# Two-block layer kernel: attention turns, exponents and casts moved; norms summed per token; a joint norm; half a gate product on ScalarE

## The reference

```python
# first block, on 16 meta tokens + x
xn = rmsnorm(h, ln1_w);  proj = xn @ w_in        # dq dk dv | gq gk gv gr | gate ranks
da = rmsnorm(softmax(q1 k1) v - lam * softmax(q2 k2) v) * 0.8          # 4 heads
go = rmsnorm(gated_linear_attention_both_ways(gq, gk, gv, g)) * silu(gr)   # 4 heads
h = h + concat(da, go) @ w_out;  h = h[16:]
hn = rmsnorm(h, ln2_w)
h = h + peer(hn)       # 8 heads pick 16 of 16384 experts per token: sum gate * gelu(hn . u) * v
x = rmsnorm(h, final_norm_w)
# second block
h = rmsnorm(x, mix_norm);  z = h @ w_in_2        # pool | u, v | two gates
y_a = (windowed means of z_pool, 2 4 8 16 wide, @ w_pool) * scale @ w_branch_a
y_b = (gelu(u) * (w_spatial @ rmsnorm(gelu(v)) + b)) @ w_branch_b
x = x + (sigmoid(g_a) * y_a + sigmoid(g_b) * y_b) @ w_out_2
x = x + conv_ffn(rmsnorm(x));  x = x + sigmoid(rmsnorm(x) @ w_ple_gate) * (p @ w_ple)
return rmsnorm(x, final_norm)
```

## Time and profile before

| | us |
|---|---|
| median of 3 runs | 2437.65 (2434.55 to 2437.88) |
| profiled execution | 2438.38 |
| its span | 2436.6 |
| mean granted clock of TensorE | 0.984 of 2.4 GHz |

### The profile page before, as it was taken

How to read it: one execution, slowest core, us unless ns; L and a number is a source line. 1 busy time by engine, 2 the same in 40 slices (tenths; PEclk the granted TensorE clock), 3 DMA queues, 4 the chain that set the end, 5 groups by cost and what they waited for, 6 DMA issues and landing times.

```text
span 2436.6 us, 38068 instructions
## 1 busy us (share of the span) xinstructions
PE 2334.8 (96%) x13568; PEld 1298.9 (53%) x13568; DVE 1700.0 (70%) x2984; ACT 1053.1 (43%) x1496; POOL 535.7 (22%) x418
## 2 busy tenths in 40 slices
PE   7999899999999998899999999988999989999998
PEld 3446774555555566655555555563444444443454
DVE  5326775578899989978888888868353447776235
ACT  4265442666666654543333333344422233332233
POOL 0001001567788631124222222104000010000001
PEclk9998999999999999999999999999999999999998
DMA  5200012487899669899999999913233323332321
GB/s 179 78 27 1 1 57 92 144 287 289 302 324 343 226 228 331 326 336 361 377 363 361 363 356 362 343 53 113 78 113 100 100 87 96 103 97 96 100 86 52
DMA packets 164871, 470.79 MB, mean 193 GB/s; under 512 B 17616, under 2 KB 70736, under 8 KB 163984
## 3 DMA queue, kind: packets, MB, share of 16 engines
q1 hardware_dynamic: 109312, 289.59, 34.9%
q0 software_dynamic: 36864, 134.23, 14.8%
q10 hardware_dynamic: 18576, 45.36, 4.9%
HBM read 421.67 MB, written 47.45 MB: 193 GB/s over the span
## 4 chain that ended last, share of the span: by engine, by line
PE 82%; DVE 12%; issue 2%; ACT 2%; DMA 1%; POOL 1%; DVEq 0%; SPq 0%; ACTq 0%; POOLq 0%
PE psum L536 25%; PE psum L537 24%; PE psum L538 24%; DVE arena L2043 2%; PE psum L426 1%; DVE arena L510 1%; DVE arena L2081 1%; DVE arena L2078 1%; DVE arena L2082 1%; PE psum L990 1%; PE psum L876 1%; PE psum L962 1%; DMA arena<-in_urows,arena 1%; PE psum L850 0%; DVE arena L2079 0%
## 5 line engine op out<-in xcount | busy, mean ns | idle before, releaser
L536 PE MATMUL psum<-arena 128*128 128x384 f16 (+2 forms) x3648 | 1261.3, 347 | 35.1 <-DVE arena L467 13.2
L537 PE MATMUL psum<-arena 128*128 128x384 f16 (+2 forms) x3648 | 1264.5, 347 | 0.0
L538 PE MATMUL psum<-arena 128*128 128x384 f16 (+2 forms) x3648 | 1257.7, 346 | 0.0
L536 PEld LDWEIGHTS psum<-arena 128*128 128x128 f16 x3648 | 354.2, 97 | 367.1 <-issue 51.2
L538 PEld LDWEIGHTS psum<-arena 128*128 128x128 f16 x3648 | 353.9, 97 | 324.0 <-issue 8.1
L537 PEld LDWEIGHTS psum<-arena 128*128 128x128 f16 x3648 | 353.6, 97 | 311.8 <-issue 8.1
L510 DVE SCALAR_TENSOR_TENSOR arena<-arena 128x1024 f16<-128x1024 f32 x216 | 268.2, 1244 | 297.6 <-ACT arena L497 297.1
L497 ACT ACTIVATE arena<-arena 128x1024 f16<-128x1024 f32 x216 | 226.1, 1050 | 255.9 <-PE psum L538 243.8
L1622 ACT ACTIVATE arena<-arena 128x1024 f16<-128x1024 f32 x128 | 135.3, 1057 | 299.8 <-PE psum L538 285.8
L516 POOL TENSOR_TENSOR arena<-arena 128x1024 f16<-128x1024 f32 x104 | 214.4, 2061 | 105.4 <-ACT arena L505 104.4
L438 POOL TENSOR_TENSOR arena<-arena 128x512 f32<-128x512 f32 x15 | 19.8, 1321 | 918.4 <-ACT arena L393 918.4
(11 more groups left out here) (251 smaller groups left out, 2179.7 us busy)
## 6 DMA issues: line engine op xcount, KB each, us to landing
arena<-in_w SPq DMA_DIRECT2D x320, 512.0 KB, 3.6
arena<-in_v SPq DMA_DIRECT2D x128, 512.0 KB, 6.0
early_activations<-arena ACTq DMA_DIRECT2D x124, 192.0 KB, 5.1
arena<-early_activations SPq DMA_DIRECT2D x124, 192.0 KB, 5.9
gate_matrix<-arena ACTq DMA_DIRECT2D x5, 4096.0 KB, 16.1
arena<-gate_matrix SPq DMA_DIRECT2D x32, 640.0 KB, 8.0
arena<-in_xT SPq DMA_DIRECT2D x4, 512.0 KB, 6.0
arena<-in_urows,arena POOLq DMA_INDIRECT x128, 6.9
```

What stands on the lines that cost most here:

```text
L536: nc.tensor.matmul(ps, a_h, b_h, start=first, stop=False)
L537: nc.tensor.matmul(ps, a_h, b_l, start=False, stop=False)
L538: return nc.tensor.matmul(ps, a_l, b_h, start=False, stop=last)
```

## The change

- Norms: the squares become the weights and a few columns the moving side, so that each token's sum lands in its own row and the result has 4 or 5 columns (`pick`). Root and reciprocal work on those; TensorE spreads the inverse by a broadcast column times the identity, now for the first norm too. There VectorE adds squares 3 to 7; one of three weight cuts goes behind the reciprocal.
- final1 and mixn are one `Norm`: with s1 and s2 the mean squares of the input and of the input times the weight, the factor of the second norm is computed from both (`wpick`, `w12`, `moments`), in one pass. Its sums for chunks 0 to 5 stand inside the last `expert_output`. The multiply that makes the first block's output X runs in the first pool projection.
- Scores, maximum, exponential and difference of turns 0 and 1 run between the gate projections. The gate is 1 + tanh(x/2) for twice the sigmoid, with the half in a later factor.
- The first two exponents use free banks (1 and 3) and run between the last turns.
- In head 0 the head norm only scales; cast and subtraction of the four heads run in the first eight steps of head 1. The wide product waits for the scaling alone.
- In the gate rows VectorE makes the low product for four of the eight tokens, ScalarE the other four with one activation each (`low_half`), for the octet ahead.
- Pool projections run from the last chunk to the first; four slabs of gating values come between them and the pool products, whose results go into U2 instead of V2.

```diff
 N_PQ = 32
 N_U = 48
 N_POOL = N_U + NK
-N_WP = N_POOL + 8
-N_SV = N_WP + 4
-N_SU = N_SV + 8
+N_SV = N_POOL + 8
+N_WP = N_SV + 4
+N_SV2 = N_WP + 4
+N_SU = N_SV2 + 4
...
-                if self.meta:
-                    nc.tensor.matmul(bank(self.b), ones, self.sq[:, c, 0:T], start=c == 0, stop=c == KC - 1)
-                    last = nc.tensor.matmul(bank(self.b + 1, M), ones, self.sq[:, c, T:TM], start=c == 0,
-                                            stop=c == KC - 1)
+                end = c == KC - 1 or c == self.lo and self.hi == KC - 1
+                for t in (0, *range(TT, self.tiles), *range(1, TT)):
+                    rows = P if t < TT else M
+                    w = wpick[:, c, 6 - 2 * t:14 - 2 * t] if self.double else pick[:, TT - t:TT - t + self.n]
+                    last = nc.tensor.matmul(bank(self.sums, self.n)[0:rows], self.squares[:, c, t * P:t * P + rows], w,
+                                            start=first and t == 0, stop=end and t == TT - 1)
+                if end:
+                    last.then_inc(ss_done, 1)
...
+            def add_squares(self, eng, op):
+                for c in range(self.lo + 1, self.hi + 1):
+                    eng.wait_ge(sq_act, self.i * KC + c + 1)
+                    if c > self.lo + 1:
+                        eng.wait_ge(squares_added, self.before + c - self.lo - 1)
+                    op.tensor_tensor(self.sq[:, self.lo, 0:self.cols], self.sq[:, self.lo, 0:self.cols],
+                                     self.sq[:, c, 0:self.cols], ALU.add).then_inc(squares_added, 1)
...
+                pe.wait_ge(inv_done, self.i + 1)
+                for at, b in ((TT, self.b), (0, self.b - 1)) if self.double else ((0, self.b),):
+                    for t in range(self.tiles):
+                        rows = P if t < TT else M
+                        last = nc.tensor.matmul(psum[:, b * 512 + t * P:b * 512 + t * P + rows],
+                                                self.inv[0:rows, at + t:at + t + 1].to_broadcast([rows, P]),
+                                                ident[0:rows, 0:rows], start=True, stop=True)
+                    last.then_inc(spread_done, 1)
...
+                if self.double:
+                    dve.wait_ge(ss_done, self.i + 1)
+                    s1, s2 = (bank(self.sums, self.n)[:, j:self.n:2] for j in range(2))
+                    dchain.link(nc.vector.tensor_scalar(moments[:, 0:TT], s1, EPS, None, ALU.add))
+                    dchain.link(nc.vector.scalar_tensor_tensor(out=moments[:, TT:2 * TT], in0=moments[:, 0:TT], scalar=EPS,
+                                                               in1=s2, op0=ALU.mult, op1=ALU.add))
+                    nc.vector.reciprocal(self.std, moments).then_inc(std_done, 1)
                 else:
...
-            return psum[0:rows, (6 + n % 2) * 512:(7 + n % 2) * 512]
+            b = 6 + n % 2 if n >= 2 else 1 + 2 * n
+            return psum[0:rows, b * 512:(b + 1) * 512]
...
+                pe.wait_ge(gate_out, 1 + (n - N_GR + 1))
+                chunk(pe, n, slot(n), bank(4 + n - N_GR))
+                if n == N_GR + 1:
+                    pe.wait_ge(proj_out, 4)
+                    scores(0)
+                elif n == N_GR + 2:
+                    scores(1)
+            for turn in range(2, HEADS * TT):
...
+            exponents(0)
+            turn_over(HEADS * TT - 1)
+            mix_values(HEADS * TT - 2)
...
+            exponents(1)
             mix_values(HEADS * TT - 1)
-            pe.wait_ge(turn_out, HEADS * TT)
-            exponents(0)
-            pe.wait_ge(av_out, HEADS)
-            exponents(1)
...
-                    pe.wait_ge(mixl_out, 1)
+                    pe.wait_ge(head_scaled, HEADS)
...
+                pe.wait_ge(low_out, e + 1)
...
+                        if c >= 2:
+                            n4.sum(pe, c - 2)
                 if not last:
...
+            pe.wait_ge(final1_out, KC)
+            gating_values(N_SV)
+            pe.wait_ge(zpool_out, KC)
+            for n in range(N_WP, N_SV2):
+                p = n - N_WP
+                g = N_SV2 - 1 - n
...
+            gating_values(N_SV2)
...
+                nc.scalar.activation(sgr[:, n - N_GR, :], bank(4 + n - N_GR), ACT.Tanh, scale=ISW / 2).then_inc(sig_out, 1)
+                if 1 <= n - N_GR <= 2:
+                    turn_exp(n - N_GR - 1)
...
+            turn_copy(HEADS * TT - 2)
             step_exp(0)
+            turn_copy(HEADS * TT - 1)
...
+            step_exp(1)
+            head_out(HEADS - 1)
...
+            def low_half(e):
+                b = e % 2
+                act.wait_ge(hot_slab_out, e + 1)
+                wait(act, g_done, e * 2 - 2)
+                for j in range(OCT // 2, OCT):
+                    tok = e * OCT + j
+                    last = nc.scalar.activation(hot_low[b][:, j // QUAD, :, j % QUAD],
+                                                hot_slab[b][:, j // QUAD, :, j % QUAD], ACT.Copy,
+                                                scale=idxT[:, 2, tok:tok + 1])
+                last.then_inc(low_out, 1)
...
+                    if t * OCT + i + 1 < GT * OCT:
+                        low_half(t * OCT + i + 1)
...
+                dve.wait_ge(sig_out, n - N_GR + 1)
+                nc.vector.scalar_tensor_tensor(out=sgr[:, n - N_GR, :], in0=sgr[:, n - N_GR, :], scalar=1.0,
+                                               in1=bank(4 + n - N_GR), op0=ALU.add,
+                                               op1=ALU.mult).then_inc(silu_out, 1)
+                if 1 <= n - N_GR <= 2:
+                    scores_max(n - N_GR - 1)
+                    difference(n - N_GR - 1)
+            for turn in range(2, HEADS * TT):
...
+                scaled = nc.vector.scalar_tensor_tensor(out=o, in0=o, scalar=w, in1=bank(h),
+                                                        op0=ALU.mult, op1=ALU.mult)
+                if k == 0:
+                    scaled.then_inc(head_scaled, 1)
+                    return
+                dchain.link(scaled)
...
+                    if h == 1 and p < 2 * HEADS:
+                        head_cut(p // 2, p % 2)
...
+                nc.vector.tensor_tensor(hot_low[b][:, 0:half], hot_slab[b][:, 0:half], col(gatel)[:, 0:half],
+                                        ALU.mult).then_inc(hot_out, 1)
             def tile_turn(t):
...
+                    dve.wait_ge(spread_done, n4.i + 2)
+                    for cc in range(KC):
+                        nc.vector.scalar_tensor_tensor(out=X[:, cc, 0:T], in0=X[:, cc, 0:T], scalar=f1[:, cc:cc + 1],
+                                                       in1=bank(n4.b - 1), op0=ALU.mult,
+                                                       op1=ALU.mult).then_inc(final1_out, 1)
...
```

More of the change, by code:

```diff
@@ L366, in build @@
         xn_done, xh_done, xl_done = sem("xn_done"), sem("xh_done"), sem("xl_done")
-        POOLED, FIRST = ("ln2", "ffnn", "final2"), 6
         squares_added = sem("squares_added")
-        NORMS = ("ln1", "ln2", "final1", "mixn", "ffnn", "plen", "final2")
+        NORMS = ("ln1", "ln2", "mixn", "ffnn", "plen", "final2")
+        ADDED = {"ln1": (3, 7), "ln2": (0, 5), "ffnn": (0, 5), "final2": (0, 5)}
         def roots_table(i):
@@ L375, in build, with __init__ @@
         class Norm:
-            def __init__(self, name, b):
+            def __init__(self, name, b, sums=None):
                 self.i = NORMS.index(name)
[L380 to L383, removed]
+                self.b, self.sums = b, b if sums is None else sums
+                self.w, self.meta, self.double = VEC[name], name == "ln1", name == "mixn"
+                self.cut = name != "final2"
                 self.cols = TM if self.meta else T
[L386 to L389, removed]
+                self.tiles = TT + 1 if self.meta else TT
+                self.n = 2 * TT if self.double else self.tiles
+                self.lo, self.hi = ADDED.get(name, (KC, KC))
+                self.before = sum(ADDED[x][1] - ADDED[x][0] for x in NORMS[:self.i] if x in ADDED)
+                self.sq = nsq1 if self.meta else nsq
+                self.squares = xsq if self.double else self.sq
+                self.std = (nstd1 if self.meta else nstd)[:, 0:self.n]
+                self.inv = (ninv1 if self.meta else ninv)[:, 0:self.n]
             def square(self, c):
-                nc.scalar.activation(self.sq[:, c, 0:self.cols], X[:, c, 0:self.cols],
+                nc.scalar.activation(self.squares[:, c, 0:self.cols], X[:, c, 0:self.cols],
                                      ACT.Square).then_inc(sq_act, 1)
@@ L412, in sum @@
                 first = c == 0
[L413 to L414 removed]
+                if self.lo <= c <= self.hi:
+                    if c < self.hi:
                         return
[L416 to L417 removed]
+                    pe.wait_ge(squares_added, self.before + self.hi - self.lo)
+                    c, first = self.lo, self.lo == 0
                 else:
@@ L2332, in _ @@
```

(2 more changed lines are left out.)

357 lines of the change are left out of this document (173 added, 184 removed).

## The result

The changed kernel takes 2412.3 us (four runs, 2406.3 to 2417.2) against 2437.7 before: ratio 0.990, interval 0.9885 to 0.991. In a second series it took 2406.9 (2405.1 to 2411.2). It is faster, by 25 to 31 us, where 53 were predicted: both medians lie above the predicted 2385 and above the end of its range (2372 to 2402). The profiled execution took 2406.3, the fastest of the first four: its span is 2404.6, 32.0 less than before.

A forecast was written before the change was run, and what follows sets the result against it. TensorE, busy 96% of the span, bounds most stages; its idle time and the slow clock behind it can be won. Terms from norms to pool order sum to -52.8 us, from 2438.4 to 2385.6, forecast 2385; range 2372 to 2402.

The forecast's parts named there:

- Norms: Root and reciprocal on few columns shorten ln2, ffnn and final2 by 0.95 us each, -2.9 together; plen 0.
- TensorE's sum costs the same, 0.23 us each: In the norms' sums, a square matrix loaded as weights with 4 columns moved is no cheaper than 128 moved.
- First norm: At the kernel's start: shorter root and reciprocal and earlier sums, less a new spread and reordered weight cuts: -4.5 us.
- early turns: Start of attention: scores 0 and 1 between gate projections make the stretch to turn 5 12.3 instead of 20.6 us: -8.
- Early exponents and first head: Gated attention: earlier exponents give -2 us; casts and subtractions leaving the first head give -7, 1.5 of 8.5 left.
- Head 1: Second head of the gated attention: the casts and subtractions moved there cost +1 us, bounds 0 and +4.5.
- rival (c): VectorE gives gains back in head 1 (4.5 us of casts) and the pool projections (4.9 of multiplies): 2393; chance 0.12.
- Gate rows: VectorE's halved low product saves 2.1 us per tile, 12.8 in six; taken as -8, bounds 0 and -12.8.
- VectorE's 31.6 becomes 29.4 to 29.5: Gate-row tile: VectorE's time falls to this many us and stays the pace, as TensorE needs 28.3 without its waits.
- Rival (a): The gate rows gain nothing, because in-order ScalarE or the transfers become their pace: 2393 us; chance 0.18.
- Joint norm: Two norms before the pool mixer become one, with sums of chunks 0 to 5 inside the last expert: -12.8 us.
- rival (b): The clock stays at 2.4 GHz after the shorter norms, where it fell before: 2375 us; chance 0.12.

The follow-up runs named there:

- The run with late turns: The changed kernel with the first two attention turns back behind the gate projections, all else kept: 2418.4 us, ratio 0.9917.
- the last kernel: Changed kernel with 128-column sums, ring at word 3974, VectorE making octet 0's whole low product, octet 4's dot product before its low cut: 2386.6 us.
- `wide`: The changed kernel with the sums of ln2, plen, ffnn and final2 moving 128 columns instead of 4: 2399.5 us; three later kernels keep this.

## Why the prediction was wrong

The direction and most mechanisms were right, 2385 was not: 27 us off the first median. By the trace, 32.0 instead of 52.8 were won. Two steps failed by most: the sum with 4 columns moved, priced like the one with 128 (6.4 us lost at plen), and the query heads, taken as untouched because their code was (5.6 lost). Two more terms were too large, the gate rows by 3.7 us and the first gated head with its exponents by 2.8. Step by step:

- *Norms:* -3.6 for ln2, ffnn and final2 together against -2.9. But "TensorE's sum costs the same, 0.23 us each" and "plen: 0" failed, and this is one of the two large errors: at plen a square matrix loaded with 4 columns moved took 12.1 us for what 128 columns did in 7.4, +6.4 with what follows. The price of a weight load came from a row at full clock. I had priced the edit by duration at a given clock, and the clock was what it changed. At ln2 and the final norm it cost too, up to 2.4 and 1.6 us by the run with 128 columns there, hidden in a part that still came out as forecast.
- *First norm* -4.1, *early turns* -7.7 in the trace against -4.5 and -8. The first is the best of the executions: in the second profile of the same program it is -2.9. The run with late turns bears the second out. Of the table loads ahead of the first exponential (1.28 us each) one is gone, as the prediction had it: the tanh left the exponential's table in place.
- *Early exponents and first head:* -5.2 for -8. VectorE did start 4.2 us earlier (its first exponent product at 241.5, before at 257.5 less the 11.8 of shift), and the casts did leave. But it then waited 5.5 us for TensorE inside the head, where it had waited 3.4, and TensorE's wait for the wide scores fell from 4.37 to 2.00 only. The "1.5 that I leave" of 8.5 had to be more: an engine that runs ahead meets the other half of the loop. Head 1 lost 0.4 (predicted 1), so rival (c) didn't come there. In the second profile it lost 3.4, because the clock fell in it.
- *Query heads:* no step of the prediction named them, and they lost 5.6. Nothing in their code changed; their addresses did.
- *Gate rows:* -4.3 for -8. Small activations cost 0.29 start to start and VectorE's half 0.33, both as estimated. The failed step is "VectorE's 31.6 becomes 29.4 to 29.5", which let its idle time stay as it was. VectorE's work did shrink by 2.1 us per tile, but its wait in order for one cut, which nobody needed yet, grew from 0.83 to 1.61, and the tile won 1.1; 2.1 us at the start, TensorE's wait for ScalarE's first half, were not in the sum at all. Rival (a) had the part at nothing, and about half of the forecast came; of its two reasons ScalarE's load was tested and fell, and the transfers did not keep the last kernel from 29.3.
- *Joint norm* -11.9 for -12.8 and *pool order* -7.2 for -8.6: both within their bounds. In the pool part waits of 1.4 and 0.7 us on VectorE appeared, as (c) had it. No run isolates these two; their sizes are read from the traces alone.
- *The clock:* rival (b) asked whether it would stay up behind the norms. It didn't behind ln2; it now does behind the two shorter waits of the attention part, but not in every execution. The prediction laid the fall to the idle time before a product, and at ln2 that is not enough: behind the same wait of 2.32 us the clock fell in every trace in which the sums moved 4 columns and held in two of the four with `wide`. This is part of the spread between runs (after 11 and 6 us in series of four, before 3 in four and 6 to 13 in series of nine to eleven), and of the 6 us between the profiled execution and the first median.

What stays open: why the start of its inputs matters to GpSimd, the 5 us that some kernels at slow addresses lose in the last two heads, why 4 columns moved bring the clock down, and why one unused word also shortened the gate rows.

The Trainium skill ("VectorE: DVE Perf Modes", "The TRN2 errata") spoke against small instructions; here four activations of 128 elements, 0.29 us apart, were worth their cost (1.1 us per tile, less 2.1 once), as ScalarE had room for them: with them it is busy 25.9 of 30.47 us.

## What to carry to other kernels

A change of the layout is a change of the kernel: compare the mean duration of instructions that you didn't touch, and if one moved, restore the addresses before you look for another cause. When an edit changes the shape of TensorE's work at the same busy time, read the granted clock over it and behind it. And where an engine is called the pace, look for its single long wait and at what it could do first; leaving load away from its neighbour tells whether load is the matter.

## What was unexpected of the hardware

- GpSimd's subtraction of 128x1024 (f32 and f16 in, f16 out) takes 2.00 or 2.12 to 2.13 us by where its two inputs begin within 16 bytes; VectorE's form of it took 1.22 us at all 34 addresses tried.
- A VectorE operation on 64 elements took 1.67 or 2.12 us instead of 0.18 and ended 0.06 us behind the GpSimd cut that ran beside it.
- 64 f32 weight loads with 4 columns moved each brought the granted clock to 0.59 with TensorE busy 98% of the time; with 128 columns it stayed at 1.00.
- The same program kept the clock at 1.00 or had 0.68 over 10 us, behind the same wait of 2 us.
